# Attention heads taken in pairs: value products of two heads in halves of TensorE's columns, scores of two heads in halves of its rows

## What is computed

```python
p = jax.nn.softmax(s1, axis=-1) - lam * jax.nn.softmax(s2, axis=-1)   # 6 differential heads, q and k of width 32 twice
s = jnp.einsum('bhgqd,bhkd->bhgqk', q, k) * scale                     # 6 grouped heads, 2 kv heads
p = jax.nn.softmax(s, axis=-1)
sm = jnp.einsum('bhsd,bhmd->bhsm', mq, mk) * HEAD_DIM ** -0.5         # 4 heads on a memory of 256 rows
y = jnp.concatenate([oa, ob, om], axis=-1) @ w_out[l]
x = x + rms_norm(y, post_norm[l])
```

## Time and profile before

| | |
|---|---|
| median of three runs | 2784.16 us (2781.27 to 2784.74) |
| the profiled execution | 2780.26 us, of which its span is 2778.5 |
| TensorE busy | 2677.9 us, 96% of the span |
| VectorE, ScalarE, GpSimd busy | 1457.0, 1098.4, 688.8 us |
| mean granted clock of TensorE | 0.985 |
| layer 0, differential, grouped, memory units (first transpose of a stage to the next's) | from 213.5 (unit 4), 270.6, 329.2 to 358.4 us |
| layer 1, the same | from 576.1 (unit 4), 633.1, 691.5 to 720.7 us |

### The profile page before, as it was taken

How to read it: one execution, slowest core, us unless ns; L and a number is a source line. 1 busy time by engine, 2 the same in 40 slices (tenths; PEclk the granted TensorE clock), 3 DMA queues, 4 the chain that set the end, 5 groups by cost and what they waited for, 6 DMA issues and landing times.

```text
span 2778.5 us, 35900 instructions
## 1 busy us (share of the span) xinstructions
PE 2677.9 (96%) x13694; PEld 2208.9 (80%) x13694; DVE 1457.0 (52%) x2028; ACT 1098.4 (40%) x1787; POOL 688.8 (25%) x601
## 2 busy tenths in 40 slices
PE   6999999989999999999999999999999998999998
PEld 6876688756888888898788888887888886888887
DVE  4576655765464432686364442565432874644423
ACT  3357643576443322323352222342222574422222
POOL 2047430274278500254120000265000100200000
PEclk9999999999999999999999999999999999999999
DMA  3320023200144323454222223355223442232232
GB/s 127 122 76 1 16 78 121 83 10 1 50 105 153 127 78 94 138 143 146 92 76 91 92 85 94 92 193 201 92 84 104 151 160 85 85 96 91 77 96 70
DMA packets 307707, 269.11 MB, mean 97 GB/s; under 512 B 44595, under 2 KB 297948, under 8 KB 303996
## 3 DMA queue, kind: packets, MB, share of 16 engines
q1 hardware_dynamic: 300780, 241.71, 28.2%
q0 software_dynamic: 2768, 20.12, 1.8%
q10 hardware_dynamic: 4032, 5.57, 0.7%
HBM read 239.60 MB, written 27.77 MB: 96 GB/s over the span
## 4 chain that ended last, share of the span: by engine, by line
PE 75%; DVE 8%; POOL 5%; issue 3%; ACT 3%; POOLq 2%; DVEq 2%; DMA 1%; SPq 1%; ACTq 0%
PE bank L419 22%; PE bank L421 22%; PE bank L420 22%; POOL E L1828 2%; POOLq L1827 2%; PE bank L1974 2%; PE bank L1316 1%; DVE XL L479 1%; DVE X L583 1%; ACT WH L381 1%; POOL MBA L794 1%; POOL MBB L794 1%; DVE work L579 1%; PE bank L1960 1%; DVEq L581 1%
## 5 line engine op out<-in xcount | busy, mean ns | idle before, releaser
L419 PE MATMUL bank<-XH,WH 128*128 128x512 f32 (+1 forms) x2400 | 900.4, 375 | 37.7 <-DVE WL L386 13.1
L420 PE MATMUL bank<-XL,WH 128*128 128x512 f32 (+1 forms) x2400 | 888.5, 370 | 0.0
L421 PE MATMUL bank<-XH,WL 128*128 128x512 f32 (+1 forms) x2400 | 888.3, 370 | 0.0
L386 DVE TENSOR_TENSOR WL<-raw,WH 128x2048 fp32r<-128x2048 f32 (+1 forms) x208 | 447.0, 2149 | 532.4 <-ACT WH L381 532.1
L419 PEld LDWEIGHTS bank<-XH,WH 128*128 128x128 f32 x2400 | 456.2, 190 | 132.6 <-DVE WL L386 18.4
L381 ACT ACTIVATE WH<-raw 128x2048 fp32r<-128x2048 f32 (+1 forms) x208 | 362.5, 1743 | 447.3 <-PE bank L421 446.8
L420 PEld LDWEIGHTS bank<-XL,WH 128*128 128x128 f32 x2400 | 456.8, 190 | 83.2 <-issue 1.9
L421 PEld LDWEIGHTS bank<-XH,WL 128*128 128x128 f32 x2400 | 455.8, 190 | 82.8
L1113 POOL TENSOR_TENSOR ssq<-ssq,sq 128x512 f32<-128x512 f32 x24 | 30.9, 1288 | 1081.0 <-ACT sq L1022 1081.0
L421 PE MATMUL bank<-HH,WL 128*128 128x512 f32 (+1 forms) x792 | 293.5, 371 | 0.0
L419 PE MATMUL bank<-HH,WH 128*128 128x512 f32 (+1 forms) x792 | 293.2, 370 | 0.0
(11 more groups left out here) (410 smaller groups left out, 3612.7 us busy)
## 6 DMA issues: line engine op xcount, KB each, us to landing
raw<-in_ffn_w_dram SPq DMA_DIRECT2D x88, 1024.0 KB, 5.3
raw<-in_ffn_w_dram SPq DMA_DIRECT2D x64, 704.0 KB, 4.6
raw<-in_w_in_dram SPq DMA_DIRECT2D x24, 1024.0 KB, 5.4
MM<-mm_scr SPq DMA_DIRECT2D x12, 1152.0 KB, 7.8
raw<-in_w_out_dram SPq DMA_DIRECT2D x8, 1024.0 KB, 5.2
raw<-in_cv_w_in_dram SPq DMA_DIRECT2D x8, 1024.0 KB, 5.5
mm_scr<-MBA POOLq DMA_DIRECT2D x6, 1152.0 KB, 4.7
mm_scr<-MBB POOLq DMA_DIRECT2D x6, 1152.0 KB, 4.4
```

The source lines that it names most:

```text
L386: dve.tensor_tensor(WL[:, slot, 0:n * P], raw[:, slot, 0:n * P], WH[:, slot, 0:n * P].bitcast(F32), ALU.subtract).then_inc(l_done, 1)
L419: pe.matmul(out, WH[:, slot, c:c + P], h, start=start, stop=False)
L420: pe.matmul(out, WH[:, slot, c:c + P], l, start=False, stop=False)
L421: return pe.matmul(out, WL[:, slot, c:c + P], h, start=False, stop=stop)
```

## The change

The heads of a pair (0 and 1, 2 and 3, ...) now alternate unit by unit, a second buffer PT1 (in the place of ML, which is not used any more at that time) holds the odd head's probabilities, and:

- **Scores.** Of grouped and memory heads, the units of both heads of a pair are issued together, in the even unit's iteration. The even head lies in rows 0 to 63, the odd in rows 64 to 127. Differential units are issued as before.
- **Values.** The values of one head are 64 columns wide, and its output goes to rows 0 to 63 or 64 to 127 of the pair's bank, so the two heads of a pair use different halves of the array's columns. Half a pair's queries are 8 (memory: 4) products, 16 (8) records, issued in two parts: part 0 behind the transposes of iteration 4n, part 1 ahead of those of iteration 4n + 1.
- **Copies.** VectorE copies the odd units of grouped heads too (`by_dve`): 24 copies in a layer, not 12. ScalarE has 40, not 52. `turned` waits for the same half of the pair before it.
- **Outputs.** One operation of 128 rows for each pair, 8 in a layer for 16 of 64 rows. `Vg` holds each head's values once, so ScalarE writes it in one instruction instead of two.

```diff
-        UNITS = [(h, t) for h in range(NHEAD) for t in range(4)]
+        UNITS = [(2 * p + i, t) for p in range(NHEAD // 2) for t in range(4) for i in range(2)]
...
-            return u < DIFF_UNITS and u % 2 == 1
+            return u < MEM_U and u % 2 == 1
...
-            def values(h, half):
-                _, v, nk, _ = HEADS[h]
-                wait_turned(pe, 4 * h + 2 * half + 1)
...
+            def values(p, half, part):
+
+                nk = HEADS[2 * p][2]
+                if part == 0:
+                    wait_turned(pe, 8 * p + 4 * half + 3)
...
                 cols = slice(256 * half, 256 * half + 256)
-                out = value_bank(h)[:, cols]
-                for c in range(nk):
-                    mm = pe.matmul(out, v(c), PT[:, c, cols], start=(c == 0), stop=(c == nk - 1))
-                mm.then_inc(ss(s, "pv"), 1)
+                for c in range(part * nk // 2, (part + 1) * nk // 2):
+                    for i in range(2):
+                        mm = pe.matmul(value_bank(p)[64 * i:64 * i + 64, cols], HEADS[2 * p + i][1](c), PTS[i][:, c, cols],
+                                       start=(c == 0), stop=(c == nk - 1))
+                if part == 1:
+                    mm.then_inc(ss(s, "pv"), 1)
...
-                if u < len(UNITS):
+                if u < DIFF_UNITS:
                     scores(u)
+                elif u < len(UNITS) and u % 2 == 0:
+                    scores(u)
+                    scores(u + 1)
                 if u in MIX_PART:
                     mix_part(*MIX_PART[u])
-                if u >= LAG_V and (u - LAG_V) % 2 == 1:
-                    values(UNITS[u - LAG_V][0], UNITS[u - LAG_V][1] // 2)
+                if u >= LAG_V and (u - LAG_V) % 4 == 3:
+                    values((u - LAG_V) // 8, (u - LAG_V) % 8 // 4, 1)
                 if LAG_T <= u < len(UNITS) + LAG_T:
                     transposes(u - LAG_T)
+                if u >= LAG_V - 1 and (u - LAG_V + 1) % 4 == 3 and u < len(UNITS) + LAG_V - 1:
+                    values((u - LAG_V + 1) // 8, (u - LAG_V + 1) % 8 // 4, 0)
```

More of the change, by code:

```diff
@@ L239, in program @@
         MH = sb("MH", [P, KD, NMEM], F32R, rb)
+        rb2 = ExitStack()
+        PT1 = sb("PT1", [P, 4, T], F32, rb2)
+        rb2.close()
         ML = sb("ML", [P, KD, NMEM], F32R, rb)
@@ L1638, in score_bank, with value_bank @@
             return bank[m % 4 if u < MEM_U else (3, 0, 1)[(m - M_MEM) % 3]]
-        def value_bank(h):
-            return bank[6 + h % 2] if h < MEM_H else bank[6]
+        def value_bank(p):
+            return bank[6 + p % 2] if p < MEM_P else bank[6]
         def slot(m):
@@ L2079, in value_high @@
                 else:
-                    for half in range(2):
-                        ins = act.activation(Vg[:, :, :, 64 * half:64 * half + 64],
-                                             b.rearrange("p (t g c) -> p t g c", t=4, g=2), ACT.Copy)
-                    ins.then_inc(ss(s, "vh"), 1)
+                    act.activation(Vg[:, :, :], b.rearrange("p (t c) -> p t c", t=4), ACT.Copy).then_inc(ss(s, "vh"), 1)
             def lead_qk(n):
@@ L2348, in sums, with outputs @@
                 ins.then_inc(ss(s, "rsum"), 1)
-            def outputs(h):
-                row = (h % 2) * 64
-                dve.wait_ge(ss(s, "pv"), at(s, "pv", 2 * h + 2))
-                acc = value_bank(h)[row:row + 64, :]
-                if h == 6:
+            def outputs(p):
+                dve.wait_ge(ss(s, "pv"), at(s, "pv", 2 * p + 2))
+                acc = value_bank(p)[:, :]
+                if p == 3:
                     dve.wait_ge(ss(s, "gate"), at(s, "gate", len(GATES)))
-                if h < 6:
-                    ins = dve.tensor_copy(PR[row:row + 64, DQ + h // 2, :], acc)
+                if p < 3:
+                    ins = dve.tensor_copy(PR[:, DQ + p, :], acc)
                 else:
-                    g = PR[row:row + 64, HEADS[h][3], :]
+                    g = PR[:, GATES[p], :]
                     ins = dve.tensor_tensor(g, acc, g, ALU.mult)
@@ L2375, in attn_dve @@
             for u in range(len(UNITS) + LAG_V + 1):
-                if u > MEM_U + LAG_V and UNITS[u - LAG_V - 1][1] == 3:
-                    outputs(UNITS[u - LAG_V - 1][0])
+                if u > MEM_U + LAG_V and (u - LAG_V - 1) % 8 == 7:
+                    outputs((u - LAG_V - 1) // 8)
                 if u < len(UNITS):
@@ L2399, in attn_dve @@
                     sums(u - 1)
-                if LAG_V < u <= MEM_U + LAG_V and UNITS[u - LAG_V - 1][1] == 3:
-                    outputs(UNITS[u - LAG_V - 1][0])
+                if LAG_V < u <= MEM_U + LAG_V and (u - LAG_V - 1) % 8 == 7:
+                    outputs((u - LAG_V - 1) // 8)
                 if NORM_U + 2 <= u < NORM_U + 5:
```

45 lines of the change are left out of this document (23 added, 22 removed).

## The result

The changed kernel takes 2785.7 us (median of 20 runs, 2783.3 to 2791.1) against 2781.3 for the kernel before on the same chip (20 runs, 2778.5 to 2786.7): ratio 1.0013, 95% interval 1.0007 to 1.0019. So it is some 4 us slower: the interval leaves out 1, but the difference is within the 0.2% that I call the same. I had forecast 2757 and a range that ends at 2785.

A forecast was written before the change was run, and what follows sets the result against it. TensorE was taken to bound grouped and memory heads, with GpSimd's floor near in the differential heads. Layer 0's -10.6 and layer 1's -17.2 us gave -28 from the median 2784.2: 2757, range 2718 to 2785.

The forecast's parts named there:

- Row and column tiles overlap: Scores and value products: paired scores merge into one slot, 16 half-width value records pass in 8 slots.
- serial halves: Rival, value products: column halves run one after the other, +15 us per layer, time 2815; chance 8%.
- strict order: Rival, TensorE: matmuls start strictly in program order, five slots for six scores, time 2775; chance 5%.
- Differential heads: Differential stage: clock falls between value products, 3.3 us per unit, +5.3 us in layer 0 and +5.5 in layer 1.
- the sign of being right: Differential heads: granted clock near 0.6 from 204 to 276, and 1.00 soon after.
- clock stays up: Rival, differential heads: 2.5 us per unit at full clock and no slow entry, time 2720; chance 16%.
- Grouped heads: Grouped stage: 48 us in layer 0, where VectorE is late, and 41 in layer 1; gains 10.6 and 17.4.
- slow entry: Start of the grouped stage: 5 us at half speed until dense work restores the clock, +2.5 us per layer.
- signs of being wrong: Differential stage under 52 or over 80 us; grouped stage over 55 us; new TensorE waits for exponents or copies.
- Memory heads: Memory stage: per pair one scores slot and half the value products go, 0.97 x 8 = 7.8 us less per layer.
- I add no wait: Memory heads: the odd unit's early scores need an earlier exponent, but about 3 us lie between, so no wait.
- I count nothing for that: Outputs and Vg: half as many outputs, and the one-instruction copy to Vg ahead of the loop, counted as no change.

The follow-up runs named there:

- second filler kernel: The filled kernel with the same filler also in iterations 42, 43, 46, 47, 50 and 51: 2750.8 us, ratio 0.9886.
- the spread kernel: Changed kernel with the differential value products moved: part 0 ahead of the transposes of iteration 4n + 1, part 1 of 4n + 3: 2781.0 us, ratio 1.0000.
- the filled kernel: Changed kernel plus half-repeated even value products, grouped copies on ScalarE, extra ScalarE copy, and filler (4 records) in iterations 5 to 8: 2749.5 us, ratio 0.9883.

## Why the prediction was wrong

- **Row and column tiles overlap:** right, both. The rivals of serial halves and of strict order are out.
- **Differential heads:** right in mechanism; that the length came out too is luck. I had 20 x 3.3 = 66 us for units 4 to 24; 64.7 and 66.4 were measured. But my 3.3 was 0.8 of the units at the low clock's 3.5 us and 0.2 at 2.5. The clock was low in about half of the stage only (31.5 of 64.7 us and 35.5 of 66.4, mean 0.76 and 0.73, not near the 0.6 that I named as the sign of being right). A unit cost 3.58 us where a run showed the low clock alone, so by my estimate the others took some 3 us each at the high clock, not 2.5, because TensorE waits there. The two errors cancel. The rival "clock stays up" described a kernel that needed filler to exist; with the clock at 1.00 the stage took 52.2 us, near that rival's 50. I took the clock as a result of the change to be borne, not as a term to be removed.
- **Grouped heads, the first step that failed:** 48 and 41 us forecast, and 2.5 of slow entry beside them; 57.8 and 49.3 measured, 7.3 and 5.8 us over. The slow entry did not come: the clock was back at 1.00 from 272.7 and 644.7, ahead of the stage. So against 48 and 41 the stage itself is 9.8 and 8.3 us too long. My own signs of being wrong were there: a grouped stage over 55 us, and new waits of TensorE for exponents and copies. I summed VectorE over the whole stage (45.8 us, measured 43.9) and took the sum for the length. Its work is not spread like that: in layer 1 it has 17.3 us of work in the 21.8 us of the last nine units, of which some 10 are norms and rests (L2375, L2377, L2382), and 15.8 in the 27.6 us of the first fifteen. Those nine units took 21.3 us before the change and 21.8 after, and never under 19.3 in any kernel, with the clock held (19.4) or not, so some 2 us were to be had there; all of layer 1's gain lies in the first 15 units (37.1 to 27.6). In layer 0 the parameter operations take the gain of these too. And the copies that the change moves to VectorE cost more than they free: 8 to 10 us by the run that puts them back on ScalarE.
- **Memory heads, the second:** "I add no wait" for the paired scores, -7.8 us per layer. Measured +0.8 and +0.7. Units 52 to 63 gained 2.6 us, but 48 to 52 lost 3.4. TensorE, ScalarE and VectorE at the first memory heads of layer 1:

```profile
699.67 0.38 PE L1935 MATMUL bank<-work2r,work1r 64*128 64x256 f32 x1 [1.03 <-ACT E L2172]
...
702.18 0.41 PE L1964 MATMUL bank<-ident,E 128*128 128x128 f32 x2 [1.90 <-issue]
702.52 3.47 PE L1980 MATMUL bank<-PT,Vg 128*64 128x256 f32 x16
705.93 0.55 PE L1964 MATMUL bank<-ident,E 128*128 128x128 f32 x2
697.25 1.91 ACT L384 ACTIVATE WH<-raw 128x2048 fp32r<-128x2048 f32 x1
699.06 0.46 ACT L2172 ACTIVATE E<-bank,stats 128x256 f32<-128x256 f32 x1
699.19 2.29 DVE L389 TENSOR_TENSOR WL<-raw,WH 128x2048 fp32r<-128x2048 f32 x1 [0.47 <-ACT WH L384]
701.40 0.68 DVE L2347 COPY PT<-bank 128x512 f32<-128x512 f32 x1
```

  The second scores of the pair wait 1.03 us for an exponent that stands behind ScalarE's rounding of weights (L384). The next transposes wait 1.90 us, by their times for the copy that the change moved to VectorE (L2347), which stands behind its subtraction for the weights (L389). Then the clock is low and 16 value records take 3.41 us (702.52 to 705.93) instead of 1.88.

  With the clock held there TensorE sets the pace again, and the stage takes 24.6 us (the second filler kernel):

```profile
320.90:345.46 24.56, 23.61 (x143) 14.68 (x143) 10.70 (x31) 14.58 (x47) 8.87 (x14) 1.00 0.13 44
```

  That is 3.7 less than the 28.3 before, so half of the 7.8 was a wrong size even then. I had 0.86 us for the value products of a pair's half, as overlapped; they are two groups of 4 half-width records (L1980), of 0.58 us each (711.04 to 711.62). Four times 0.31 us more makes 1.2 of the 4.1 that are missing; for the rest I have no cause.
- **"I count nothing for that", the third:** the copy to `Vg` that became one instruction moved the start by 3.4 us in layer 0 and 1.0 in layer 1, and undoing that gave 8.
- **Sum.** My terms give 2784.2 - 27.8 = 2756.4, which I wrote as 2757. Missing against the forecast: 13.1 us in the grouped heads, 17.1 in the memory heads (twice 7.8 and the 1.5 by which they grew), 5.5 up to the fourth unit, less 0.9 in the differential heads: 34.8, which takes -27.8 to +7.0. The spans differ by 6.5, the medians by 4.4.

The falls of the clock came after waits of 1.14 us (in the kernel before) to 2.00 us. But in the spread kernel the clock stayed down for 44 us with hardly a gap, and the filled kernel bore a wait of 1.9 us at 2.4 GHz:

```profile
PE bank L1972 <- POOL E L1833: 4.4, 7, 1.9
```

(its waits from 200 to 262: us in total, times, longest). The rule that I weighed, that long idle gaps between bursts of matmuls lose the clock (the Trainium skill, TensorE: Matmul & The Clock Gate, "Why this matters for your kernels"), is thus not the whole of what decides here: no wait in these rows was longer than 2.00 us, and what TensorE does between the waits mattered as much as their length.

Inside the units 24 to 39 of layer 1 one more term was too small. They take 27.6 us at 2.4 GHz. 15 groups of transposes at 0.58, 7.5 pairs of scores at 0.90 and 4 groups of value products at 1.88 make 23.0 (I had 21.5), and the waits for GpSimd 2.0. The other 2.6 are products of the norms (L1945), which stand between the transposes of 671.72, 0.58 us long, and the next scores:

```profile
672.21 1.88 PE L1945 MATMUL bank<-sq,perm 128*128 128x512 f32 x4
673.93 1.02 PE L1945 MATMUL bank<-ssq,perm 128*128 128x512 f32 x2
674.88 0.49 PE L1935 MATMUL bank<-work2r,roper 64*128 64x512 f32 x1
```

What stays open: what sets the 19.3 us of the units 39 to 48, which no kernel went under, and whether the filler would do without the repeats. Nor was the filler tried in the changed kernel as it stands, without the other edits.

## What to carry to other kernels

When another engine sets the pace of a stage, work taken off TensorE is not free time: its clock can fall to half, and then it is TensorE that sets the pace again, slower than before. Look for the waits that the halved work leaves, and fill them, off the critical order, before calling the change a failure. And sum an engine's load over the stretch in which its work is dense, not over the stage; a stage's mean hid the nine units in which nothing could be gained.

## What the runs showed of the hardware

- Products in different column halves pass two at a time: 16 records in 1.88 us against 8 in 1.83. Products of two units in different row halves do so as well, though issued three apart.
- The clock stayed at 1.2 GHz for 44.2 us while TensorE's records covered 43.1 of them, with groups of 8 half-width value records between scores and transposes; with such a group in every iteration it returned to 2.4 GHz after 17 us and stayed for 41. A busy share of TensorE near 1 in the profile is thus no proof of a high clock.
- Half-width products one after the other cost as much as wide ones and a little more: 1.87 us for 8 instead of 1.83, 1.01 for 4 shorter ones instead of 0.86, and 8 us for the kernel.
- VectorE's two additions of 128 x 512 took 2.40 us instead of 1.29 while GpSimd's subtraction ran, and 36 small operations of VectorE 17.2 us among the differential heads, where GpSimd is busy, instead of 8.4 among the grouped ones.
